# Sums of squares of q and k in a forgetting attention: one fp32 product each, or two products of split squares

## The reference, cut to what matters

```python
def rms_norm(x, g):
    xf = x.astype(jnp.float32)
    y = xf * lax.rsqrt(jnp.mean(xf * xf, axis=-1, keepdims=True) + EPS)
    return (y * g.astype(jnp.float32)).astype(x.dtype)

def fox_mixer(h, w_in, b_f, q_gain, k_gain, w_out):
    b_, s_, _ = h.shape
    proj = h @ w_in
    q, k, v, g, f_logit = jnp.split(proj, [FOX_WIDTH, 2 * FOX_WIDTH, 3 * FOX_WIDTH, 4 * FOX_WIDTH], axis=-1)
    log_f = jax.nn.log_sigmoid(f_logit.astype(jnp.float32) + b_f.astype(jnp.float32))
    qh = rms_norm(to_heads(q, FOX_HEADS), q_gain)
    kh = rms_norm(to_heads(k, FOX_HEADS), k_gain)
    vh = to_heads(v, FOX_HEADS)
    o = fox_attention(qh, kh, vh, log_f.transpose(0, 2, 1))
    o = o.transpose(0, 2, 1, 3).reshape(b_, s_, FOX_WIDTH)
    return (o * jax.nn.silu(g)) @ w_out
```

## Time and profile before

| | us |
|---|---|
| median of three runs | 1547.44 |
| the three runs | 1540.58, 1547.44, 1548.29 |
| the profiled execution, its own time | 1539.76 |
| the profiled execution, its span | 1538.0 |
| one loop turn of the forgetting attention (from one `og` of head 0 at 1154.11 to the next at 1190.40) | 36.3 |

### The profile page before, as it was taken

The page is one execution under the profiler, slowest core; times in us unless marked ns, Lnnn a source line. Parts: engine busy times, 40 slices in busy tenths (PEclk is TensorE's granted clock), DMA queues, the critical chain, the costliest instruction groups (busy, mean ns, idle before and its releaser), DMA issues.

```text
span 1538.0 us, 18015 instructions
## 1 busy us (share of the span) xinstructions
PE 1412.2 (92%) x6912; PEld 1182.8 (77%) x6912; DVE 949.0 (62%) x1324; ACT 711.9 (46%) x940; POOL 81.7 (5%) x81
## 2 busy tenths in 40 slices
PE   4798889999989999999979999999789999996996
PEld 3687777888868888888868898787667777775875
DVE  6798786444354444444478776536776677777365
ACT  4677767332232223232346444335365666556251
POOL 3000000000300000000020000021100000000202
PEclk9999999999989999999989999999899999997998
DMA  5111011322212232322221121222121111111211
GB/s 191 56 55 56 1 55 55 110 90 101 105 60 84 108 108 82 109 82 101 91 82 55 55 107 58 96 85 108 55 82 55 55 55 55 55 55 69 82 55 55
DMA packets 19237, 118.16 MB, mean 77 GB/s; under 512 B 2400, under 2 KB 3680, under 8 KB 5616
## 3 DMA queue, kind: packets, MB, share of 16 engines
q1 hardware_dynamic: 18896, 116.38, 21.3%
q0 software_dynamic: 288, 1.05, 0.2%
HBM read 115.32 MB, written 2.10 MB: 76 GB/s over the span
## 4 chain that ended last, share of the span: by engine, by line
PE 64%; DVE 17%; ACT 12%; issue 6%; DVEq 0%; DMA 0%; ACTq 0%
PE ps L500 20%; PE ps L502 19%; PE ps L501 19%; DVE wlo L1598 2%; ACT whi L1046 1%; PE ps L683 1%; ACT fq L1046 1%; PE ps L953 1%; ACT fka L1046 1%; DVE acc L376 1%; DVE att L1843 1%; DVE nmax L2166 1%; PE ps L564 1%; ACT pthi L1046 1%; ACT att L1165 1%
## 5 line engine op out<-in xcount | busy, mean ns | idle before, releaser
L500 PE MATMUL ps<-uhi,whi 128*128 128x512 f32 x1168 | 466.7, 400 | 12.4 <-DVE ulo L1647 6.0
L502 PE MATMUL ps<-uhi,wlo 128*128 128x512 f32 x1168 | 457.8, 392 | 0.0
L501 PE MATMUL ps<-ulo,whi 128*128 128x512 f32 x1168 | 457.4, 392 | 0.0
L1598 DVE TENSOR_TENSOR wlo<-wraw,whi 128x2048 fp32r<-128x2048 f32 x105 | 240.2, 2290 | 109.2 <-ACT whi L1046 107.6
L1046 ACT ACTIVATE whi<-wraw 128x2048 fp32r<-128x2048 f32 x105 | 200.4, 1908 | 182.2 <-PE ps L502 182.0
L500 PEld LDWEIGHTS ps<-uhi,whi 128*128 128x128 f32 x1168 | 221.4, 190 | 65.2 <-issue 15.8
L502 PEld LDWEIGHTS ps<-uhi,wlo 128*128 128x128 f32 x1168 | 220.8, 189 | 47.5
L501 PEld LDWEIGHTS ps<-ulo,whi 128*128 128x128 f32 x1168 | 221.7, 190 | 45.3 <-issue 1.9
L500 PE MATMUL ps<-hdhi,whi 128*128 128x512 f32 x256 | 99.6, 389 | 0.0
L501 PE MATMUL ps<-hdlo,whi 128*128 128x512 f32 x256 | 99.6, 389 | 0.0
L502 PE MATMUL ps<-hdhi,wlo 128*128 128x512 f32 x256 | 99.6, 389 | 0.0
(11 more groups left out here) (391 smaller groups left out, 2354.8 us busy)
## 6 DMA issues: line engine op xcount, KB each, us to landing
wraw<-wstream SPq DMA_DIRECT2D x105, 1024.0 KB, 4.7
h<-xT SPq DMA_DIRECT2D x4, 512.0 KB, 5.5
outT<-pp SPq DMA_DIRECT2D x8, 256.0 KB, 2.2
s5b<-s5p_d SPq DMA_DIRECT2D x1, 1024.0 KB, 12.1
pe_in<-pT POOLq DMA_DIRECT2D x2, 512.0 KB, 3.6
cst_in<-cst_d SPq DMA_DIRECT2D x5, 64.0 KB, 10.2
reset<-cst_d SPq DMA_DIRECT2D x1, 256.0 KB, 11.4
ones<-cst_d SPq DMA_DIRECT2D x1, 64.0 KB, 2.6
```

The costliest lines, as they stand in the source:

```text
L500: nc.tensor.matmul(out, lh, rh, start=start, stop=False, skip_group_check=True)
L501: nc.tensor.matmul(out, lh, rl_, start=False, stop=False, skip_group_check=True)
L502: mm = nc.tensor.matmul(out, ll, rh, start=False, stop=stop, skip_group_check=True)
L1598: V.tensor_tensor(wlo[:, slot, :], wraw[:, slot, :], whi[:, slot, :], ALU.subtract).then_inc(lo_done, 1)
```

## The change

The squares stay (`qksq`). ACT then casts them to fp32r as `sqhi`, right behind the squares and ahead of whatever stood next. DVE subtracts and stores `sqlo`. PE waits for `sqlo` and makes two fp32r matmuls with `headonesr` for q and two for k, in place of one fp32 matmul each. `headonesr` is an fp32r copy of `headones`, made once on DVE in `fox_prepare`. `sqlo` shares its memory with `f_t`, and `qksq` with `f_half`. Aside from this, one semaphore of the state-space layer at the kernel's start is dropped: a reciprocal of 128x16 on DVE signals the engine's own counter, and GpSimd no longer waits for it.

```diff
@@ memory
-                qksq = sb("qksq", [P, 2, T], F32, s)
+                sqhi = sb("sqhi", [P, 2, T], F32R, s)
+                with scope() as z:
+                    sqlo = sb("sqlo", [P, 2, T], F32R, z)
+                    qksq = sb("qksq", [P, 2, T], F32, z)
...
+                headonesr = sb("headonesr", [P, P], F32R, s)
@@ GpSimd, s5_powers
-                pool.wait_ge(s5_inv, 1)
@@ PE
             def fox_qk_sums(i):
-                pe.wait_ge(qk_sq, i + 1)
+                pe.wait_ge(sq_lo, i + 1)
                 for k in range(2):
-                    mm = nc.tensor.matmul(ps[:, Z0 + k, :], headones[:, :], qksq[:, k, :], start=True, stop=True)
+                    nc.tensor.matmul(ps[:, Z0 + k, :], headonesr[:, :], sqhi[:, k, :], start=True, stop=False)
+                    mm = nc.tensor.matmul(ps[:, Z0 + k, :], headonesr[:, :], sqlo[:, k, :], start=False, stop=True)
                 mm.then_inc(qk_ss, 1)
@@ ACT
             def fox_squares(i):
                 act.wait_ge(qk_copy, i * 2 + 2)
                 A(qksq[:, :, :], qk[:, :, :], ACT.Square).then_inc(qk_sq, 1)
+                act.wait_ge(qk_sq, i + 1)
+                copy(sqhi[:, :, :], qksq[:, :, :]).then_inc(sq_hi, 1)
@@ DVE, s5_prepare
-                V.reciprocal(r[20], r[21]).then_inc(s5_inv, 1)
+                own.do(V.reciprocal(r[20], r[21]))
@@ DVE
             def fox_prepare():
                 own.do(V.tensor_scalar(gq8[:, :], vec("fox_q_norm"), 0.125, None, ALU.mult))
+                own.do(V.tensor_copy(headonesr[:, :], headones[:, :]))
...
+            def fox_squares_lo(i):
+                dve.wait_ge(sq_hi, i + 1)
+                V.tensor_tensor(sqlo[:, :, :], qksq[:, :, :], sqhi[:, :, :], ALU.subtract).then_inc(sq_lo, 1)
...
                 row_max(1)
                 normalise(1)
+                if not last:
+                    fox_squares_lo(i + 1)
...
             fox_prepare()
+            fox_squares_lo(0)
             fox_qk_norm(0)
```

More of the change, by code:

```diff
@@ L323, in build @@
         h_normed = sem("h_normed")
-        s5_exp, s5_arg, s5_trig, s5_inv = sem("s5_exp"), sem("s5_arg"), sem("s5_trig"), sem("s5_inverse")
+        s5_exp, s5_arg, s5_trig = sem("s5_exp"), sem("s5_arg"), sem("s5_trig")
+        sq_hi, sq_lo = sem("fox_squares_hi"), sem("fox_squares_ready")
         q_hi, qk_ready, vT_ready, uch_ready = sem("qk_hi"), sem("qk_ready"), sem("vT_ready"), sem("u_ssm_ready")
```

## The result

The changed kernel takes 1560.79 us in the median of six executions (1558.59 to 1566.03). The kernel before took 1547.29 us beside it (six executions, 1540.58 to 1548.29). The ratio is 1.0100 with a 95% interval from 1.0083 to 1.0118: **slower by 13.5 us, 1.0%**. The profiled execution took 1560.17 us, with a span of 1558.0.

The account below looks back on a forecast made before the run. The prediction took a closed chain through ACT, PE and DVE to bound the loop, not PE. Terms 5.1 + 4.9 + 3.4 = 13.4 us slower gave 1553.2 from the profile, 1560.8 from the median; forecast 1557 between, range 1546 to 1567.

Parts of the forecast that it names:

- What bounds the kernel: Loop turn of 36.3 us: one closed chain through ACT, PE and DVE; PE's saved 0.81 us per pair counts nothing.
- The passes: PE's sums: four fp32r matmuls, 0.23 us each in the loop, 0.43 apart ahead of it at half clock.
- The copy ahead of `og`: ACT in the loop: the sqhi copy delays og by 0.73 us in each of seven turns, 5.1 us.
- `sqlo` in the loop, covered: DVE in the loop: the 1.21 us subtraction fits into idle time, PE's need covered by 0.5 us; no cost.
- Ahead of the loop: sqlo(0) queues behind scan and logarithm, so f_t starts 4.0 us later; 4.9 us with sums at half clock.
- The cover of PE's gemm: Ahead of the loop: PE's 48-matmul gemm of 10.9 us fits before fvT, about half a microsecond thin.
- The dropped semaphore at the start: Kernel's start: GpSimd's dropped wait concerns a 128x16 reciprocal that was already over; costs nothing.
- The clock in the loop: PE's wait ahead of head 0's transposes grows to 2.0 us; falls in two of six turns, 1.7 us each, 3.4 us.
- The clock falls in nearly each turn: Rival, 8%: the loop's clock term is 10.2 us, total 20.2 us slower, 1560 to 1568 us.
- the worst case: Upper bound of the loop's clock term: 10.2 us, with 1.7 us for each fall in six turns.
- The base: Starting time for the sum: 1543.6 us, the middle of the profiled 1539.76 and the median 1547.44.
- the third rival: Only one of the two places, loop or ahead of it, is in the chain: 4 to 5 us, 1544 to 1553; 12%.

Follow-up runs that it names:

- e6: Changed kernel with both halves of the squares made on DVE, pair 0's ahead of the wait for the logarithm, no cast on ACT; 1555.36 us, ratio 1.0058.
- e12: e6 plus matmuls nobody reads in PE's waits: 7 a turn ahead of head 0's transposes, 14 ahead of the loop; 1546.94 us, ratio 0.9997.
- e9: e6 with DVE writing the next pair's gate bias earlier, ahead of the squares' halves; 1541.90 us, ratio 0.9973.
- e10: Kernel before, fp32 sums kept, with only the next pair's gate bias moved earlier on DVE; 1546.87 us, ratio 1.0002.
- e3: Kernel before plus only ACT's cast of the squares to sqhi, read by nobody; PE's sums stay fp32; 1554.26 us, ratio 1.0049.
- e2: Changed kernel with the sqhi cast moved behind og, the store of head 0, on ACT; 1551.92 us, ratio 1.0046.
- e1: Changed kernel with DVE making pair 0's sqlo before it waits for ACT's logarithm, not after the scan; 1556.32 us, ratio 1.0076.
- e4: Kernel before with only the semaphore edit at the start: GpSimd's wait for the 128x16 reciprocal dropped; 1545.92 us, ratio 0.9998.
- e5: Changed kernel without the low half: ACT writes squares straight as fp32r, PE makes two passes instead of four; 1555.89 us, ratio 1.0065.

## Why the prediction was right, and where it was off

The forecast of 1557 us is 3.8 below the median, the range of 1546 to 1567 holds it, and the sign was right. Step by step:

- **What bounds the kernel.** The reading that the loop is one closed chain through ACT's `og`, PE's transposes and DVE, and not PE's 92%, held: the changed kernel saves PE's 0.81 us and gets none of it. Cheaper matmuls on the 92% engine are worth nothing in e6's first two turns and in e12 against before, and 0.76 us a turn only in e9 against e10, after DVE's chain is shortened. The Trainium skill (Perfetto Trace Analysis, Identifying the Most-Contended Engine) would have one optimize the engine of highest occupancy first, and judge TensorE by its weight loads rather than its matmul time; both name PE here (77% and 92%, DVE 62%), and neither tells that a saving on it stays without effect in this loop.
- **The passes.** Predicted 0.23 apart in the loop and 0.43 ahead of it; measured 0.23 to 0.31, and 0.43 to 0.59, the first being the longest each time.
- **The copy ahead of `og`, 5.1 us.** Predicted 0.73 us a turn, and PE's wait for `og` at 1.6; measured 37.0 - 36.28 = 0.72 and 1.57. e3 shows it alone. Right.
- **`sqlo` in the loop, covered.** PE never waited for it in the changed kernel. e2 shows what the cover hid: 0.83 us as soon as the copy comes later.
- **Ahead of the loop, 4.9 us.** Measured 5.02, with the wait of 8.0 us as forecast (7.97), and 4.2 with the clock held (predicted 4.0). e1 shows that 3.85 of it hang on the scan. The cover of PE's gemm that the prediction called half a microsecond thin held: PE's wait for `fvT` behind it went from 2.9 us to 0.2, and `fvT` came 5.0 us later, no more than `f_t`. Right.
- **The dropped semaphore at the start, nothing.** e4: nothing.
- **The clock in the loop, 3.4 us.** Two falls, as I had put down, but 1.3 and 1.2 us each and not 1.7: PE falls behind by 1.31 us from the transposes to the gemm. The 1.7 took the whole 3.4 us of a low stretch for work that takes twice as long, and for work on which the turn waits. The number of falls was right by luck. e1 has the same loop and had four, e6 and e5 had five and six at the same wait of 1.9 us. "The clock falls in nearly each turn" deserved far more than 8%; my argument that 2.0 us lies nearer to the waits of 1.2 and 1.77 us that did no harm than to the 3.24 that did took the length of the wait for what decides. The trace of before has rows in between and beyond that the prediction left out: PE waited 2.32 us at 25.27, 2.11 at 983.47, 2.92 at 1133.91, 3.26 at 20.88 and 3.45 at 54.96, each with a granted clock of 1.00 behind it. The longest of them, and the stretch behind it:

```profile
54.96 1.09 PE L597 MATMUL ps<-ident,ET 128*128 128x128 f32 x8 [3.45 <-DVE ET L1726]
...
55.00:58.40 3.40, 3.40 (x29) 3.32 (x29) 1.91 (x3) 1.24 (x2) 0.00 (x0) 1.00 0.00 0
```

So no length of wait parted the harmless from the harmful even there. What the price of the worst case is, the runs also tell: 7 x 1.3 = 9 us, and not 10.2 for six turns.
- **The Trainium skill on the clock** (TensorE: Matmul & The Clock Gate, What's actually happening): the throttled rate as the default, which activity has to release. In the loop the runs agree: e5 takes activity away and falls to half clock six times (granted clock 0.54 to 0.58 behind the wait), e12 puts it back and stays at 1.00.
- **The base.** I placed it at 1543.6, halfway between the profiled 1539.76 and the median of 1547.44. Of all steps this one was furthest off, by 3.7 us: the medians of before in the jobs lie at 1545.7, 1546.5, 1546.8 and 1547.3, and the profiled execution was an early one of a spread that e4 shows in the start. The sum of 13.4 on the median gives 1560.8, and the measured median is 1560.79; that they agree this well is partly chance, since the term for the falls was 0.9 too large, and how many falls the other five executions had is not known.
- **The range.** Its lower end, 1546, is called the middle of the third rival, which as written (1544 to 1553) has its middle at 1548.5. Nothing else hangs on it.

What stays open: why the same wait of 1.9 us is followed by half clock in some turns and not in others. Over the changed kernel, e1, e5 and e6 it was in 17 of 24 turns; behind waits of 1.0 to 1.5 us at that place it never was. A part of an answer lies in the times at which the falls begin: within one execution they keep an even spacing, 37.54 to 37.56 us in e5, e6 and once in e1, and 75.09 us, twice as much, between the two falls of the changed kernel and twice in e1. In e5 and e6 a turn with a fall takes 37.6 to 37.75 us; in the changed kernel and e1 a turn with a fall and one without take 75.3 to 75.4 together. Both lie close to the spacing, so that the same place of the turn meets the next fall. That this decides whether a wait is followed by a fall fits these profiles but is not shown; no run varied the length of the wait, or its place, in small steps.

## What to carry to other kernels

A saving on the busiest engine is worth nothing while another chain sets the turn, and the work that pays for it lands on an engine that may be in that chain: look at what stands right behind the place where the new instruction goes, on its own engine. In a step outside of the loop ask what the new instruction is queued behind; a copy and a subtraction there cost 5.0 us, as much as all seven turns, and 3.85 of it only because the subtraction stood behind a scan that waits for a logarithm. And when work leaves PE, read the length of its waits afterwards and put a price on the clock.

## What the runs showed of the hardware that I had not expected

- Taking matmuls away made a kernel 9 us slower (e5, 1555.89 against 1546.77), and adding idle ones took 8.7 us of excess from one (e12, 0.2 us over before, against e6, 8.8). Behind 17 of 24 waits of 1.9 us ahead of the transposes the clock fell to half for some 3.4 us; behind the waits of 1.0 to 1.2 us at the same place (before, e3, e9, e10) it did not.
- The falls come at an even spacing that is not the loop's: 37.54 or 37.55 us apart in e6, whose turns took 37.6 to 37.75, and likewise in e5.
- A kernel starts its last attention up to 10 us earlier or later from one execution to the next: the squares of pair 0 at 1116.98 in before and at 1127.29 in e3, with the same code ahead of them.
- DVE casts 128x1024 to fp32r in 0.69 us (e6), where ACT takes 1.06.
